# A decoder layer's output product on one core: the prompt's products in upper and rest parts

## What is computed

```
mix = (merge[..., 0, :] * (o_nsa @ w_br_nsa) + merge[..., 1, :] * (o_dil @ w_br_dil)) @ w_out
x = x + mix
h = rms_norm(x, norm_ffn).reshape(b * t, d)
return x + hier_moe(h, rg_w, rg_b, re_w, re_b, w_up, w_down).reshape(b, t, d)
```

## Time and profile before

| | |
|---|---|
| median of 3 runs | 1147.04 us (1146.37 to 1147.55) |
| the profiled execution | 1149.66 us |
| its span | 1147.8 us |
| mean granted TensorE clock | 0.953 of full speed |
| TensorE busy | 1046.5 us (91%), 8408 matmuls |
| VectorE / ScalarE / GpSimd busy | 476.7 (42%) / 310.8 (27%) / 148.2 us (13%) |
| DMA | 291 GB/s of HBM read and written over the span |
| shares of the chain that ended last | DMA of `w_up` 10%, L3115 6%, L3138 2% |

### The profile page before, as it was taken

One profiled execution on the slowest core, in us unless ns is written; L12 is line 12 of the kernel. 1 busy time (PEld: TensorE's weight loads), 2 busy tenths in 40 slices (PEclk: granted clock), 3 DMA queues, 4 the chain that ended last, 5 costly groups with the idle time before them and its releaser, 6 DMA issues. The chain is left out here.

```text
span 1147.8 us, 20576 instructions
## 1 busy us (share of the span) xinstructions
PE 1046.5 (91%) x8408; PEld 782.3 (68%) x8408; DVE 476.7 (42%) x985; ACT 310.8 (27%) x678; POOL 148.2 (13%) x188
## 2 busy tenths in 40 slices
PE   6999999999889989887999999999998999798785
PEld 6999999999856667765888878776546433233231
DVE  5443433333267744533565857525126111110105
ACT  4100000321246633322555454611111111110103
POOL 0260000600025510000111000000001112101200
PEclk9999999999979987897999999999997999998989
DMA  8423460779399992697454353329906899999966
GB/s 255 156 97 128 148 196 7 236 250 309 100 325 334 337 323 72 209 339 271 174 220 175 129 211 148 115 74 328 413 20 264 332 425 423 422 425 423 424 270 247
DMA packets 100175, 279.92 MB, mean 244 GB/s; under 512 B 17572, under 2 KB 73792, under 8 KB 88704
## 3 DMA queue, kind: packets, MB, share of 16 engines
q1 hardware_dynamic: 90048, 229.57, 55.1%
q0 software_dynamic: 6976, 42.48, 9.7%
q10 hardware_dynamic: 3072, 6.75, 1.5%
HBM read 264.52 MB, written 69.53 MB: 291 GB/s over the span
## 5 line engine op out<-in xcount | busy, mean ns | idle before, releaser
L3115 PE MATMUL ex_up_ps<-ex_w_up,ex_hT 128*64 128x512 f32 x512 | 122.9, 636 | 27.5 <-DMA ex_w_up<-in_expert_w_up 26.3
L124 PE MATMUL proj_acc<-w_in_upper,hT_upper 128*128 128x328 f32 x352 | 112.5, 320 | 2.6 <-DVE hT_rest L118 2.3
L126 PE MATMUL proj_acc<-w_in_upper,hT_rest 128*128 128x328 f32 x352 | 110.5, 314 | 0.0
L3115 PEld LDWEIGHTS ex_up_ps<-ex_w_up,ex_hT 128*64 128x64 f32 x512 | 41.3, 146 | 97.7 <-issue 87.2
L125 PE MATMUL proj_acc<-w_in_rest,hT_upper 128*128 128x328 f32 x252 | 79.8, 317 | 0.0
L124 PE MATMUL sn_hp<-sn_xT,cmp_w_upper 128*128 128x256 f32 x256 | 75.8, 296 | 0.0
L124 PE MATMUL proj_acc<-hT_upper,merge_w_upper 128*128 128x272 f32 x256 | 74.3, 290 | 1.3 <-ACT qT_dil L561 1.3
L125 PE MATMUL proj_acc<-hT_rest,merge_w_upper 128*128 128x272 f32 x256 | 73.6, 288 | 0.0
L126 PE MATMUL proj_acc<-hT_upper,merge_w_rest 128*128 128x272 f32 x256 | 73.5, 287 | 0.0
L125 PE MATMUL sn_hp<-sn_xT,cmp_w_upper 128*128 128x256 f32 x256 | 72.5, 283 | 0.0
L126 PE MATMUL sn_hp<-sn_xT,cmp_w_rest 128*128 128x256 f32 x256 | 72.4, 283 | 0.0
(11 more groups left out here) (533 smaller groups left out, 1996.6 us busy)
## 6 DMA issues: line engine op xcount, KB each, us to landing
ex_w_up<-in_expert_w_up SPq DMA_DIRECT2D x30, 2048.0 KB, 29.5
ex_w_down<-in_expert_w_down SPq DMA_DIRECT2D x32, 1024.0 KB, 28.9
out_dil_sample<-in_cache_dil_w SPq DMA_DIRECT2D x8, 4088.0 KB, 28.8
sd_kv_g<-in_cache_dil_w SPq DMA_DIRECT2D x32, 512.0 KB, 8.3
w_in_chunk<-in_w_in SPq DMA_DIRECT2D x10, 1312.0 KB, 5.9
merge_w<-in_w_in SPq DMA_DIRECT2D x16, 512.0 KB, 6.1
out_dil_sample<-in_cache_dil_w SPq DMA_DIRECT2D x8, 1016.0 KB, 8.6
merge_gates_scratch<-qT_dil ACTq DMA_DIRECT2D x16, 272.0 KB, 4.4
```

What stands on the lines that cost most here:

```text
L124: pe.matmul(out, a[0], b[0], start=first, stop=False)
L126: return pe.matmul(out, a[1], b[0], start=False, stop=last)
L3115: ins = pe.matmul(up_ps[r, q, :], hT[:, q, c, r], wu[slot][:, u, c, :], start=c == 0, stop=c == KD - 1)
```

## The change

All of it is in `mix()` but the places of `w_out`.

- **Products.** `residual(n, ks)` now takes a list of blocks k, and the late half of `w_out` (k = 4 to 7) comes first. A prompt product (n = 1 to 8) is 8 times `product_of_parts`, so 24 matmuls of 512 columns. The sample rows keep `mx_mixT` as float32 but are multiplied with the upper part and then with the rest of the matrix, both read as float32: 8 matmuls for each k instead of 4. The order is: late half of n = 1, n = 0 whole, soon half of n = 1, late half of n = 2, the transposes of the sample rows, soon half of n = 2, router, n = 3 and on. The other transposes of `h` stand ahead of n + 1 as before.
- **Splits.** ScalarE casts each block of `mx_mixT` (512 prompt columns) to `mx_mixT_upper`, and each block of `w_out` (128 x 1024) to its upper part: blocks 4 to 7 of `w_out` between the blocks 4 to 7 of the mix, behind a wait for both loads of `w_out`; blocks 0 and 1 ahead of block 7 of the mix, and 2 and 3 behind it. POOL subtracts for `w_out` blocks 4 to 7, 0 and 1, VectorE for the mix (block m - 1 behind the addition of block m) and for `w_out` blocks 2 and 3. The rests lie in the place of the whole values; the upper part of the mix lies over `mx_ahead`, that of the soon half of `w_out` over a branch matrix, and that of the late half in the place of `w_up` of expert 3.
- **Loads.** The late half of `w_out` is loaded ahead of the soon half. `w_up` of expert 3 and `w_down` of pair 2 leave the early loads; behind the last product now stand `w_up` of pair 1, `w_up` of pair 2 and `w_down` of pair 2.
- **Semaphores.** Several are joined: the gain, the router's inputs and the routing constants are counted by one, so that VectorE's first addition waits for all six. POOL's memset of `mx_mixT`'s last 96 columns waits for the sample product.

```diff
@@ mix(): places of the parts @@
+            mix_rest = self.parts_place("mx_mixT_rest", [P, KD, (NT + 1) * P])
             mixT = h2T = self.sb(s, "mx_mixT", [P, KD, (NT + 1) * P])
-            wo = [self.sb(s, "mx_w_out", [P, KD // 2, D]), wo_late]
+            slot = 4 * STRIDE // 2 * 4 * KVD
+            mix_upper = nc.alloc_sbuf_tensor_at("mx_mixT_upper", [P, 2, KD, AHEAD], F32R, offset=self.sn_raw_at + 2 * slot)
+            wo_upper = [nc.alloc_sbuf_tensor_at("mx_w_out_upper", [P, HK, D], F32R, offset=self.sn_raw_at + slot), wo_late[2]]
+            wo_rest = [self.parts_place("mx_w_out_rest", [P, HK, D]), wo_late[1]]
+            wo = [self.sb(s, "mx_w_out", [P, HK, D]), wo_late[0]]
...
@@ mix(): SyncE @@
-                    for half in range(2):
+                    for half in (1, 0):
                         sp.dma_start(wo[half][:, :, :], w_out[:, half * HK:(half + 1) * HK, :]).then_inc(s_wo, 16)
...
                     self.load_w_down(sp, wd, 1, (2, 3))
-                    self.load_w_down(sp, wd, 2, (4, 5))
-                    self.load_w_up_of(sp, wu, 1, 1, 3)
...
-                    self.load_w_up_of(sp, wu, 1, 0, 2)
+                    self.load_w_up(sp, wu, 1, (2, 3))
                     self.load_w_up(sp, wu, 2, (4, 5))
+                    self.load_w_down(sp, wd, 2, (4, 5))
...
@@ mix(): TensorE @@
+                    def w_out_ready(k):
+                        if k >= HK:
+                            pe.wait_ge(s_sp, k - HK + 1)
+                        elif k < 2:
+                            pe.wait_ge(s_sp, HK + k + 1)
+                        else:
+                            pe.wait_ge(s_sd, KD + k - 1)
+
+                    def residual(n, ks):
                         if n >= 3:
                             pe.wait_ge(s_xr, n - 2)
-                        for k in range(KD):
+                        for k in ks:
+                            if n <= 1:
+                                w_out_ready(k)
+                            first, last = k == HK, k == HK - 1
+                            parts_of_w = wo_upper[k // HK][:, k % HK, :], wo_rest[k // HK][:, k % HK, :]
                             if n == 0:
-                                pe.wait_ge(s_v, k + 1)
                                 for j in range(4):
-                                    ins = pe.matmul(ps[32 * j:32 * j + 32, 0, 0:QT], mixT[:, k, TP:T],
-                                                    wo[k // HK][:, k % HK, j * QT:(j + 1) * QT], start=k == 0, stop=k == KD - 1)
+                                    cols = slice(j * QT, (j + 1) * QT)
+                                    for part in range(2):
+                                        ins = pe.matmul(ps[32 * j:32 * j + 32, 0, 0:QT], mixT[:, k, TP:T],
+                                                        parts_of_w[part][:, cols].bitcast(F32),
+                                                        start=first and part == 0, stop=last and part == 1)
                                 continue
+                            pe.wait_ge(s_sd, k + 1)
                             t, half = divmod(n - 1, 2)
-                            ins = pe.matmul(ps[:, n % 3, :], mixT[:, k, t * P:(t + 1) * P],
-                                            wo[k // HK][:, k % HK, half * 512:(half + 1) * 512], start=k == 0, stop=k == KD - 1)
-                        ins.then_inc(s_mt, 1)
+                            cols = slice(half * 512, (half + 1) * 512)
+                            a, at = divmod(t * P, AHEAD)
+                            ins = product_of_parts(pe, ps[:, n % 3, :],
+                                                   (mix_upper[:, a, k, at:at + P], mix_rest[:, k, t * P:(t + 1) * P]),
+                                                   (parts_of_w[0][:, cols], parts_of_w[1][:, cols]), first, last)
+                        if ks[-1] == HK - 1:
+                            ins.then_inc(s_mt, 1)
...
-                    pe.wait_ge(s_wo, 32)
-                    pe.wait_ge(s_r, KD)
-                    residual(0)
+                    late, soon = list(range(HK, KD)), list(range(HK))
+                    pe.wait_ge(s_r, 2 * KD)
+                    residual(1, late)
+                    residual(0, late + soon)
+                    residual(1, soon)
                     for t in range(NT):
-                        residual(2 * t + 1)
-                        if t == NT - 1:
-                            residual(2 * t + 2)
+                        if t == 0:
+                            residual(2, late)
+                            transposes(0)
+                            residual(2, soon)
+                        elif t == NT - 1:
+                            residual(2 * t + 1, late + soon)
+                            residual(2 * t + 2, late + soon)
                             transposes(t)
                         else:
+                            residual(2 * t + 1, late + soon)
                             transposes(t)
-                            residual(2 * t + 2)
+                            residual(2 * t + 2, late + soon)
                         if t == 0:
-                            pe.wait_ge(s_router, 80)
+                            pe.wait_ge(s_in, 96)
...
@@ mix(): GpSimd @@
-                    pool.wait_ge(s_v, KD)
+                    for j in range(HK + 2):
+                        half, c = (1, j) if j < HK else (0, j - HK)
+                        pool.wait_ge(s_u, uppers["w", half * HK + c])
+                        rest_part(pool, wo_rest[half][:, c, :], wo[half][:, c, :], wo_upper[half][:, c, :]).then_inc(s_sp, 1)
+                    pool.wait_ge(s_mt, 1)
                     pool.memset(h2T[:, :, T:(NT + 1) * P], 0.0).then_inc(s_pad, 1)
-                    pool.wait_ge(s_router, 80)
+                    pool.wait_ge(s_in, 96)
...
@@ mix(): ScalarE @@
+                    def mix_upper_of(m):
+                        act.wait_ge(s_v, m + 1)
+                        act.copy(mix_upper[:, :, m, :], mixT[:, m, 0:TP].rearrange("p (a t) -> p a t", a=2)).then_inc(s_u, 1)
+
+                    def w_out_upper(half, c):
+                        act.copy(wo_upper[half][:, c, :], wo[half][:, c, :]).then_inc(s_u, 1)
+
+                    for m in range(KD):
+                        if m >= HK:
+                            if m == HK:
+                                act.wait_ge(s_wo, 32)
+                            w_out_upper(1, m - HK)
+                        if m == KD - 1:
+                            act.wait_ge(s_p[0], KD)
+                            w_out_upper(0, 0)
+                            w_out_upper(0, 1)
+                        mix_upper_of(m)
+                    w_out_upper(0, 2)
+                    w_out_upper(0, 3)
...
@@ mix(): VectorE @@
+                    def split_mix(m):
+                        dve.wait_ge(s_u, uppers["mix", m])
+                        halves = [part.rearrange("p (a t) -> p a t", a=2) for part in (mix_rest[:, m, 0:TP], mixT[:, m, 0:TP])]
+                        rest_part(dve, halves[0], halves[1], mix_upper[:, :, m, :]).then_inc(s_sd, 1)
...
+                        if m > 0:
+                            split_mix(m - 1)
+                    split_mix(KD - 1)
+                    for c in range(2, HK):
+                        dve.wait_ge(s_u, uppers["w", c])
+                        rest_part(dve, wo_rest[0][:, c, :], wo[0][:, c, :], wo_upper[0][:, c, :]).then_inc(s_sd, 1)
...
@@ decoder_layer(): places of w_out @@
-        w_out = p.place_at("mx_w_out_late", [P, KD // 2, D])
+        w_out = (p.place_at("mx_w_out_late", [P, KD // 2, D]), p.parts_place("mx_w_out_late_rest", [P, KD // 2, D]),
+                 p.parts_place("mx_w_out_late_upper", [P, KD // 2, D], skip=4 * KD // 2 * D))
```

More of the change, by code:

```diff
@@ L2749, in rms @@
                         else:
[L2750 removed]
+                            act.wait_ge(s_rms, 2 * i)
                         if i >= 3:
@@ L2781, in _ @@
                         gates = self.gates[m // HK][:, :, m % HK, :]
-                        dve.tensor_tensor(pr[:, :, 0:AHEAD], self.ahead[:, :, m, :], gates[:, :, 0:AHEAD], ALU.mult).then_inc(s_a, 1)
+                        dve.tensor_tensor(pr[:, :, 0:AHEAD], self.ahead[:, :, m, :], gates[:, :, 0:AHEAD], ALU.mult).then_inc(s_r, 1)
                         for p in range(2):
@@ L2825, in _ @@
                     dve.wait_ge(s_x, 16 * (NT + 1))
-                    dve.wait_ge(s_gain, 16)
+                    dve.wait_ge(s_in, 96)
                     add(0)
@@ L2840, in _ @@
                     copy_hT(NT)
-                    dve.wait_ge(s_router, 80)
+                    dve.wait_ge(s_in, 96)
                     dve.wait_ge(s_l, 1)
```

45 lines of the change are left out of this document (26 added, 19 removed).

## The result

| | before | changed |
|---|---|---|
| median | 1146.7 us (4 runs, 1144.1 to 1147.6) | 1162.9 us (4 runs, 1160.4 to 1169.5) |
| ratio | | 1.0162, 95% interval 1.0135 to 1.0189 |
| profiled execution, span | 1149.66, 1147.8 | 1161.7, 1159.5 |

The forecast was 1166.7 (range 1150 to 1172), slower with a chance of 0.83. The direction and the mechanism were right; of the sum's terms those of the mixing stage were too large and those of the gather too small, as the traces show.

The account below looks back on a forecast made before the run. It took the start of the first expert pair to set the end, with full DMA engines behind it. 13.4 (stage) + 2.0 (clock) + 3.3 (gather) + 1.0 (clock behind it) = 19.7 over 1147.04 gave 1166.7; range 1150 to 1172.

Parts of the forecast that it names:

- stage with all waits, sample products and parts: Mixing stage on TensorE: 21.9 us later by waits and sample products, less 8.6 saved on prompt products; ends 13.4 later.
- clock in that stage: TensorE rests from 790 to 799.5 and in pieces until 807, so its clock drops: 2.0 us, bounds 0 and 4.
- routing: Between the mixing stage and the gather of token rows; the forecast sum has no term for a change here.
- gather: POOL's first gather of token rows, beside the late weight loads, takes 7.9 instead of 4.6: +3.3 us, bounds 0 and 6.
- clock behind the gather: A longer rest of TensorE before the first pair slows its work: +1.0 us, bounds 0 and 1.8.
- TensorE's start: First product behind the branch products at 799.5 instead of 790.9, with two-tile operations of POOL and DVE excluding one another.
- Rival C: In the splits, POOL and DVE don't hold each other up: 11.1 us slower, 1158.1; chance 0.08.
- E: Splits hide, late half of n = 1 ends at 795.7, TensorE hardly cools: 4.4 us faster, 1142.6; chance 0.13.
- Sample products: Sample rows on TensorE, two products for one, only pairs overlap: 1.73 us per k, 13.8 for eight instead of 3.5.
- rival B: Sample products' column groups overlap freely, 0.87 us per k: 12.7 us slower in sum, 1159.7; chance 0.25.
- Prompt products: Each prompt product on TensorE takes 5.44 us, 1.43 saved; 8.6 us on the six products n = 3 to 8.
- Loads: 10.5 MB instead of 6.3 behind the last store of h: in time for pair 2, but the first gather meets it.

Follow-up runs that it names:

- e3_no_pool_rests: Changed kernel, but GpSimd subtracts only 32 of 1024 columns in its six operations and products read the upper part instead of those rests; 1153.8 us.
- e5_rests_on_dve: Changed kernel with GpSimd's six subtractions given to VectorE; 1154.6 us, ratio 1.0074 to before.
- e4_part_outer: Changed kernel with the sample products' loops over column groups and parts exchanged: four groups with the upper part, then four with the rest; 1164.2 us.
- e1_late_loads: Kernel before with only the changed kernel's loads: w_up of expert 3 and w_down of pair 2 behind the last store of h; 1153.1 us, ratio 1.0051.
- e2_hold: Changed kernel with the last 4.2 MB of late loads (w_up of expert 5, w_down of pair 2) issued only when the first gather has landed; 1157.5 us.
- e7_before_relaxed: Kernel before, but the sample product waits for VectorE's PSUM reading of block 4 instead of block 7; 1144.2 us, ratio 0.9983.
- e9_all: Changed kernel with e5_rests_on_dve, e6_halves, e8_interleaved and e2_hold together, w_down of experts 4 and 5 rescheduled; 1141.5 us, ratio 0.9961 to before.
- e6_halves: Changed kernel, but ScalarE waits for one half of w_out at a time, the late half ahead of block 4; 1160.7 us.
- e8_interleaved: Changed kernel with sample products of blocks 4 to 7 each behind the same block's prompt product and the wait for block 7 relaxed; 1161.5 us.

## Why the prediction was right

By its own steps, changed against before, in us:

| step | forecast | measured |
|---|---|---|
| stage with all waits, sample products and parts | +13.4 | +9.6, clock included |
| clock in that stage | +2.0 | (in the row above) |
| routing | 0 | -3.6 |
| gather | +3.3 | +5.6 |
| clock behind the gather | +1.0 | +2.2 (0.8 in the transposes, 1.4 in the up products) |
| sum | 19.7 | 13.8 in the trace; 16.2 and 18.4 by the medians |

- **TensorE's start.** Forecast at 799.5, so 32.0 us behind the first load of before; measured 31.35. The step by step walk with two-tile operations of VectorE and GpSimd excluding one another held, and the times of VectorE in e3_no_pool_rests and e5_rests_on_dve confirm it (0.7 us with GpSimd idle). The walk's 8.6 us for GpSimd running freely beside VectorE was not measured; e3's 11.7 are those of GpSimd's work left out. The Trainium skill (SBUF — State Buffer, Who interferes with whom) calls the contention an exclusive lock, and the trace agrees: 2.1 to 2.8 us instead of 0.7, and 0.74 for the product from PSUM. Rival C falls, and with it E: the faster outcome needed both that and `w_out` by 785, and it landed 19.9 us into the section, 787.4 in the time of before.
- **Sample products.** This term was wrong. I took 1.73 us per block from a program order that lets only pairs overlap; the trace shows 0.87 (rival B), each group taking its own two products one behind the other beside the other groups, and e4_part_outer that their order in the list doesn't matter. The term should have been 7.0 us for the eight blocks at full clock (7.1 in e5_rests_on_dve), not 13.8. The Trainium skill (TensorE: Matmul & The Clock Gate, The mechanism) has matmuls start and end in program order, and the forecast followed it. The trace does not agree for products in different column groups: four upper products start ahead of the first rest, which the list has second (811.35 against 811.78).
- **Clock in the stage.** The 2.0 were about right: 1.1 us in the sample products (8.2 against 7.1) and 0.8 in block 7 (1.55 us from 805.27, 0.79 for a block at full clock from 814.99).
- **Prompt products.** 5.67 us each instead of 5.44: the six give 7.2 us back, not 8.6.
- **Loads.** The queue of 10.5 MB was in time for pairs 1 and 2, as held, and it met the gather, as forecast; the price was mis-sized, 5.6 instead of 3.3, because the row it came from the earlier trace rows had met one refill, and not a full queue. The forecast did not see the products that TensorE runs ahead of the first pair; the 4.6 us of before happened to end just behind them, so that all that was added is on the path. And the faster routing made the gather meet more of the queue (10.2 us, 8.9 in e1_late_loads). e1_late_loads and e2_hold show the cause from both sides.
- **Routing.** Not foreseen. The changed kernel gained 3.6 us because its clock was full where that of before had fallen: the last 16 router products took 1.95 us instead of 3.60. From the end of the stage to the gather's issue the two profiles of before took 23.6 and 22.4 us, e1_late_loads 24.0, e7_before_relaxed 22.9, e9_all 23.2; the two of the changed kernel and e4_part_outer 19.9 to 20.0. But e2_hold, with the changed kernel's stage, took 22.7 (clock 0.50 in 870 to 880), e6_halves 22.7 and e8_interleaved 21.9, so this gain is not a sure part of the change.

The total came within 4 us of the median although the trace's own sum is 6 below it: the sample term was too large, the gather's too small, a gain in the routing was left out, and about 3 us stand in the medians that no step explains. The sign and the mechanism were derived; the nearness is in part luck.

## What to carry to other kernels

Before work is given to a second engine, ask whether it can run beside the first at all: here two-tile subtractions on GpSimd stretched VectorE's from 0.7 to 2.8 us, and giving them all to VectorE shortened the stage by 8.8 us. Weights that are loaded late do not only have to be in time for their own reader; a small gather in the same microseconds pays for them (4.6 to 10.2 us), and holding back the last 4 MB until it has landed brought it back to 4.4, of which 3.1 us reached the end in the trace. A saving on TensorE of 1.2 us per product is real, but it begins to count only when the splits, their order and their waits (one half of a matrix at a time) keep TensorE supplied: e9_all, with all of that, turns 1.6% slower into 0.4% faster.

## What the runs showed of the hardware that I had not expected

- Products of 32 rows and 256 float32 columns in four column groups run side by side, each group at 0.43 us for one of its own (0.108 us each over the four). Those of different groups do not start in the order of the list: with upper and rest in turn for each group, the four upper products start first (811.35) and the four rests 0.43 us later.
- Beside a full queue of weights (0.97 to 1.01 DMA share) the gather of the first token rows took 8.6 to 10.3 us, the less the longer the queue had run; it took 4.4 to 4.6 us with the last 4 MB held back.
- TensorE's granted clock was 0.53 to 0.62 in 790 to 810 us in the kernels in which TensorE had rested 8.9 us there, and was full again from 810 to 870. In those in which it had been at 1.00 since 780 it fell where the last prompt product ends (ten-microsecond windows of 0.57 in before, 0.50 in e1_late_loads, 0.53 in e9_all), and the work behind took 22.4 to 24.0 us. An early fall does not always spare the late one: e2_hold had both and took 22.7. What sets the place of the second fall is open.
